# Half-size products of Strassen's scheme in the out-projection and the MLP of a decode-step kernel

## What is computed

```
x = x + gate1 * (concat(pool_out, attn_out) @ w_out)          # w_out 1024 x 1024
h2 = rmsnorm(x, g_mlp) * (1 + scale2) + shift2
x = x + gate2 * (square(relu(h2 @ w_up)) @ w_down)            # 1024 x 4096, 4096 x 1024
y = rmsnorm(x, g_final)
```

## Time and profile before

| | us |
|---|---|
| median of 3 runs (1449.72 to 1454.08) | 1452.13 |
| span of the profiled execution | 1451.2 |
| TensorE (PE) busy | 1406.3 |
| VectorE (DVE) busy | 692.3 |
| ScalarE (ACT) busy | 397.4 |
| GpSimd (POOL) busy | 373.8 |

### The profile page before, as it was taken

One profiled execution on the slowest core, in us unless ns is written; L12 is line 12 of the kernel. 1 busy time (PEld: TensorE's weight loads), 2 busy tenths in 40 slices (PEclk: granted clock), 3 DMA queues, 4 the chain that ended last, 5 costly groups with the idle time before them and its releaser, 6 DMA issues.

```text
span 1451.2 us, 25502 instructions
## 1 busy us (share of the span) xinstructions
PE 1406.3 (97%) x10814; PEld 1283.6 (88%) x10814; DVE 692.3 (48%) x1358; ACT 397.4 (27%) x875; POOL 373.8 (26%) x278
## 2 busy tenths in 40 slices
PE   6999999999989998999999999999999999999998
PEld 4899876667667766999999999999999999999997
DVE  4846655655657776476532332322323323223245
ACT  5521655555413333323301102011021020110244
POOL 0032042222312217110614306025051060330400
PEclk9999989999979999999999999999999999999999
DMA  9612234234657755400211203003021030120102
GB/s 350 258 51 61 93 103 139 96 112 144 191 210 255 248 205 150 159 16 15 75 43 51 66 1 102 15 16 101 1 73 44 1 103 15 44 73 1 44 15 110
DMA packets 93920, 139.65 MB, mean 96 GB/s; under 512 B 14027, under 2 KB 65175, under 8 KB 89575
## 3 DMA queue, kind: packets, MB, share of 16 engines
q1 hardware_dynamic: 83701, 95.74, 20.6%
q0 software_dynamic: 5760, 37.75, 7.3%
q10 hardware_dynamic: 4346, 4.54, 1.0%
HBM read 121.98 MB, written 13.79 MB: 94 GB/s over the span
## 4 chain that ended last, share of the span: by engine, by line
PE 89%; DVE 4%; DMA 3%; issue 2%; ACT 1%; POOL 0%; SPq 0%; DVEq 0%; ACTq 0%
PE psa L1263 26%; PE psa L1277 26%; PE psa L1241 6%; PE psa L795 4%; PE psa L1135 4%; PE psa L979 3%; PE psa L861 3%; PE psa L1185 3%; PE psa L1017 2%; PE psa L1000 2%; DMA wm<-in_w_mod 2%; PE psa L400 1%; PE psa L876 1%; PE psa L1167 1%; PE psa L918 1%
## 5 line engine op out<-in xcount | busy, mean ns | idle before, releaser
L1263 PE MATMUL psa<-hhi,wr 128*128 128x384 f32 (+1 forms) x1536 | 374.5, 326 | 0.0
L1263 PEld LDWEIGHTS psa<-hhi,wr 128*128 128x128 f32 x1536 | 270.8, 188 | 0.1
L1277 PE MATMUL psa<-g_hi,wd_hi 128*128 128x384 f32 (+1 forms) x768 | 251.3, 327 | 0.0
L1263 PE MATMUL psa<-hlo,wr 128*128 128x384 f32 (+1 forms) x768 | 250.3, 326 | 0.0
L1277 PE MATMUL psa<-g_hi,wd_lo 128*128 128x384 f32 (+1 forms) x768 | 250.3, 326 | 0.0
L1277 PE MATMUL psa<-g_lo,wd_hi 128*128 128x384 f32 (+1 forms) x768 | 250.2, 326 | 0.0
L2184 DVE SCALAR_TENSOR_TENSOR xT<-psa,modT,xT 128x384 f32<-128x384 f32 (+1 forms) x216 | 123.1, 571 | 191.8 <-PE psa L1277 160.6
L1703 ACT ACTIVATE g_relu<-psa 128x384 f32<-128x384 f32 (+1 forms) x96 | 45.4, 473 | 600.9 <-PE psa L1263 600.9
L590 POOL TENSOR_SCALAR wr<-wraw 128x1024 fp32r<-128x1024 f32 x33 | 34.8, 1054 | 558.1 <-PE psa L1263 487.9
L2248 DVE TENSOR_TENSOR psa<-psa,g_relu 128x384 f32<-128x384 f32 (+1 forms) x96 | 52.2, 543 | 261.7 <-ACT g_relu L1703 261.7
L1263 PEld LDWEIGHTS psa<-hlo,wr 128*128 128x128 f32 x768 | 144.1, 188 | 0.1
(11 more groups left out here) (305 smaller groups left out, 2225.1 us busy)
## 6 DMA issues: line engine op xcount, KB each, us to landing
wmod<-in_w_mod SPq DMA_DIRECT2D x8, 2048.0 KB, 8.5
wraw<-in_w_up SPq DMA_DIRECT2D x32, 512.0 KB, 4.1
wraw<-in_w_down SPq DMA_DIRECT2D x32, 512.0 KB, 3.5
wm<-in_w_mod SPq DMA_DIRECT2D x4, 2048.0 KB, 19.5
x_scr<-xT SPq DMA_DIRECT2D x1, 4352.0 KB, 19.6
wraw<-in_w_out SPq DMA_DIRECT2D x8, 512.0 KB, 4.2
out_y_p<-yst SPq DMA_DIRECT2D x8, 512.0 KB, 2.6
xstage<-in_x_prompt SPq DMA_DIRECT2D x3, 1024.0 KB, 10.5
```

Of the source, the lines that this page charges most:

```text
L1263: mm = pe.matmul(out[:, :N], w[:, c * P:c * P + P], x[:, c, c0:c0 + N], start=(c == 0 and q == 0), stop=(c == KD - 1 and q == 2))
L1277: mm = pe.matmul(out[:, :N], w[:, c, n * P:n * P + P], x[:, c, c0:c0 + N], start=(c == 0 and q == 0), stop=(c == FG - 1 and q == 2))
```

## The change

The out-projection and the MLP become nine stages of the same size: stage 0 is the out-projection, and then four times an up stage (1024 of the 4096 columns) and a down stage. Each stage is a product of a 1024 x 1024 weight block and a 1024 x 1088 activation block, done by one level of Strassen's scheme in Winograd's form: the weights in four quarters of 512 x 512, the activations in two halves of rows and two token halves of 544 (`HT`). Seven products M1 to M7 of quarters (some of them sums of quarters) take the place of eight. Each product is a phase of four steps, one for each 128 rows of the half-size contraction; a step is 24 matmuls with 272 columns (`HB`): two token quarters, four output tiles, three products of high and low parts. The eight output tiles of a phase fill all eight PSUM banks. M2, M1 and M5 open new sums; M6, M7 and M4 go on from M1, and M3 from M5, in the same banks, after the sum so far was read.

For every step, a piece of weights (128 x 512) and a piece of activations (128 x 544) are made anew: `w_sum` on POOL forms the sum of weight quarters where the product wants one, `w_high` on ACT the high part, `w_low` on POOL the low part; `x_sum` on DVE, `x_high` on ACT and `x_low` on DVE do the same for the activations. All of `w_sum`, `w_low`, `x_sum` and `x_low` read two SBUF operands. There are four slots for the high and low parts: the high part of step j waits until step j - 4 is done. The sums run one step ahead of the low parts in POOL's and DVE's lists.

After each phase its eight tiles are read (`kept`): in the even stages (out, down) by `residual` on DVE; in the odd ones (up) by ACT (`first_kept`, after M2, M6, M7 and M4) or by `added` on DVE (after M1, M5 and M3), into `g_all`, which `activated` on DVE then turns into relu squared in place. In DVE's list the reading of a phase stands behind the low parts of the first three steps of the next phase. Each unit of the next phase's first step waits for the reading of its bank. The old functions `split_wo`, `split_up`, `split_down`, `wo_unit`, `up_unit`, `down_unit`, `cat_high`, `cat_low`, `norm_high`, `norm_low`, `up_high` and `relu_low` go. The norm between stage 0 and stage 1 works by token halves instead of by three blocks, and the final norm, the last turns and the stores are arranged anew for tiles of 64 to 120 tokens. Weights are loaded as whole quarters of 1 MB. The core of the diff, with the new functions:

```
+HT, HB = T // 2, T // 4
+STAGES = 9
+STEPS = 28
+EARLY = ('M2', 'M1', 'M6', 'M7', 'M4', 'M5', 'M3')
+LATE = ('M5', 'M3', 'M1', 'M6', 'M7', 'M4', 'M2')
+ORDERS = (LATE,) + (EARLY,) * (STAGES - 2) + (LATE,)
+OPENS = ('M2', 'M1', 'M5')
+TARGET = {'M2': (0, 0), 'M1': (0, 0), 'M6': (0, 1), 'M7': (1, 1), 'M4': (1, 0), 'M5': (1, 1), 'M3': (0, 1)}
+W_SUMMED = [('M5', 'M3', 'M7') if o is LATE else ('M6', 'M7', 'M5', 'M3') for o in ORDERS]
...
+X_SUMMED = ('M5', 'M6', 'M7', 'M4')
...
+    def tail_bank(p, i):
+        return bank(i if p else 4 + i)
...
+            before = w - 2 if name == 'A12' else w - 1
+            if before >= 0:
+                sp.wait_ge(sem("w_low"), STEPS * before + 4 * LAST_USE[name][before] + 4)
+            k = quarter_slot(w, name)
+            sp.dma_start(quarters[k][:, :, :], src).then_inc(sem(f"quarter_in{k}"), 16)
...
+        def w_sum(j):
+            w, pos, k, m = place(j)
+            if m not in W_SUMMED[w]:
+                return
+            a11, a12, a21, a22 = (w_quarter(w, name, k) for name in ('A11', 'A12', 'A21', 'A22'))
+            s2 = s2_sum[:, k, :]
+            if ORDERS[w] is LATE:
+                if m == 'M5':
+                    s = g.tensor_tensor(s2, a21, a22, ALU.add)
+                elif m == 'M3':
+                    chain(g.tensor_tensor(s2, s2, a11, ALU.subtract))
+                    s = g.tensor_tensor(s4_tmp[:, k % 2, :], a12, s2, ALU.subtract)
+                else:
+                    s = g.tensor_tensor(a11, a11, a21, ALU.subtract)
+            elif m == 'M6':
+                chain(g.tensor_tensor(s2, a11, a21, ALU.subtract))
+                s = g.tensor_tensor(s2, a22, s2, ALU.subtract)
+            elif m == 'M7':
+                s = g.tensor_tensor(a11, a11, a21, ALU.subtract)
+            elif m == 'M5':
+                s = g.tensor_tensor(a21, a21, a22, ALU.add)
             else:
+                s = g.tensor_tensor(s2, a12, s2, ALU.subtract)
+            s.then_inc(sem("w_sum"), 1)
+        def w_low(j):
+            if place(j)[3] in W_SUMMED[place(j)[0]]:
+                g.wait_ge(sem("w_sum"), BEFORE["w_sum"] + W_SUMS[j])
+            g.wait_ge(sem("w_high"), j + 1)
+            g.tensor_tensor(w_lo[j % 4][:, :], w_piece(j), w_hi[j % 4][:, :].bitcast(F32), ALU.subtract).then_inc(sem("w_low"), 1)
...
+            for q, (a, x) in enumerate(products(w_hi[s], w_lo[s], x_hi[s], x_lo[s])):
+                mm = pe.matmul(tail_bank(p, i)[:, 0:HB], a[:, i * P:i * P + P], x[:, HB * p:HB * p + HB],
+                               start=(m in OPENS and k == 0 and q == 0), stop=(k == 3 and q == 2),
+                               skip_group_check=True)
...
+        def step(j, p):
+            phase, k = j // 4, j % 4
+            pe.wait_ge(sem("w_low"), j + 1)
+            pe.wait_ge(sem("x_low"), j + 1)
+            for i in range(4):
+                if k == 0 and phase:
+                    pe.wait_ge(sem("unit_kept"), 8 * (phase - 1) + unit_rank(phase - 1, p, i) + 1)
+                if k == 0 and p == 0 and i >= 2 and phase in (6, 8):
+                    pe.wait_ge(sem("n_root"), phase // 2 - 2)
+                mm = unit_part(j, p, i)
+                if k == 3:
+                    mm.then_inc(sem("unit_mm"), 1)
...
+        def total(n):
+            pe.wait_ge(sem("n_sum"), n + 1)
+            pe.wait_ge(sem("unit_kept"), 8 * (6 + 2 * n))
+            for e in range(2):
+                c0 = HT * n + HB * e
+                mm = pe.matmul(bank(6 + e)[:, 0:HB], ones[:, :], h_all[:, 0, c0:c0 + HB], start=True, stop=True)
...
+        for j in range(4, 4 * (7 * STAGES - 1)):
+            if j == 24:
+                total(0)
+            if j == 32:
+                total(1)
+            step(j, 1)
+            mm = step(j, 0)
+            if j % 4 < 3:
+                mm.then_inc(sem("step_mm"), 1)
...
+        def w_high(j):
+            w, pos, k, m = place(j)
+            if j >= 4:
+                wait_step(act, j - 4)
...
+            act.activation(w_hi[j % 4][:, :], w_piece(j), ACT.Copy).then_inc(sem("w_high"), 1)
...
+            act.activation(x_hi[j % 4][:, :], x_piece(j), ACT.Copy).then_inc(sem("x_high"), 1)
...
+        def first_kept(phase):
+            for n in range(8):
+                out, c, c0, u = unit_tile(phase, n)
+                act.wait_ge(sem("unit_mm"), u + 1)
+                act.activation(g_all[:, c, c0:c0 + HB], out[:, 0:HB], ACT.Copy).then_inc(sem("unit_kept"), 1)
...
+            if j % 4 == 3 and w % 2 and m in ('M2', 'M6', 'M7', 'M4'):
+                first_kept(phase)
...
+        def x_sum(j):
...
+            if m == 'M5':
+                s = tt(x_piece(j), b12, b11, ALU.subtract)
+            elif m == 'M6':
+                chain(tt(t2, b22, b12, ALU.subtract))
+                s = tt(t2, t2, b11, ALU.add)
+            elif m == 'M7':
+                s = tt(x_piece(j), b22, b12, ALU.subtract)
+            else:
+                s = tt(t2, b21, t2, ALU.subtract)
+            s.then_inc(sem("x_sum"), 1)
...
+        def x_low(j):
+            if place(j)[3] in X_SUMMED:
+                v.wait_ge(sem("x_sum"), X_SUMS[j])
+            v.wait_ge(sem("x_high"), j + 1)
+            tt(x_lo[j % 4][:, :], x_piece(j), x_hi[j % 4][:, :].bitcast(F32), ALU.subtract).then_inc(sem("x_low"), 1)
...
+        def residual(phase, n):
+            w = phase // 7
+            out, c, c0, u = unit_tile(phase, n)
+            N, gate = HB, (M_G2 if w else M_G1) + c
+            if phase:
+                v.wait_ge(sem("unit_kept"), u - 7)
+            if c0 == TP + TS - HB:
+                N = HB - TS
+                if u:
+                    v.wait_ge(sem("unit_kept"), u)
+                new = xT[:, c, TP:T].rearrange("p (b s) -> p b s", b=NB)
+                gates = modT[:, gate, 1:9].unsqueeze(2).to_broadcast([P, NB, NS])
+                chain(tt(tmp_s[:, :, :], out[:, N:HB].rearrange("p (b s) -> p b s", b=NB), gates, ALU.mult))
                 tt(new, new, tmp_s[:, :, :], ALU.add)
+            v.scalar_tensor_tensor(out=xT[:, c, c0:c0 + N], in0=out[:, 0:N], scalar=modT[:, gate, 0:1], in1=xT[:, c, c0:c0 + N],
+                                   op0=ALU.mult, op1=ALU.add).then_inc(sem("unit_kept"), 1)
...
+        def added(phase, n):
...
+            tt(g_all[:, c, c0:c0 + HB], out[:, 0:HB], g_all[:, c, c0:c0 + HB], ALU.add).then_inc(sem("unit_kept"), 1)
...
+        def activated(phase, i):
...
+            v.scalar_tensor_tensor(out=cols, in0=cols, scalar=0.0, in1=cols, op0=ALU.max, op1=ALU.mult).then_inc(sem("g_done"), 1)
...
+        def kept(phase):
...
+            for n in range(8):
+                if w % 2 == 0:
+                    residual(phase, n)
+                elif m in ('M1', 'M5', 'M3'):
+                    added(phase, n)
...
+        for j in range(4, STAGES * STEPS):
+            phase = (j - 7) // 4
+            w, m = phase // 7, ORDERS[phase // 7][phase % 7]
+            if j % 4 == 3:
+                kept(phase)
+                if phase in (7 * STAGES - 9, 7 * STAGES - 8):
+                    for i in range(4):
+                        activated(phase, i)
+            if j % 4 < 2 and j >= 8:
+                phase = (j - 8) // 4
+                w, m = phase // 7, ORDERS[phase // 7][phase % 7]
+                if phase not in (7 * STAGES - 9, 7 * STAGES - 8) and w % 2 and m in ('M1', 'M4', 'M5', 'M3'):
+                    activated(phase, 2 * (j % 4))
+                    activated(phase, 2 * (j % 4) + 1)
+            if j in (25, 33, 249):
+                add_squares({25: 0, 33: 1, 249: 2}[j])
+            if j == 35:
+                x_low(35)
+                inverse(1)
+                sample_scale(v, chain, h_all[:, :, TP:T], xT[:, :, TP:T], rr[:, TP - HT:HT], A2, M_SH2).then_inc(sem("h_samples"), 1)
+                for c in (4, 0, 5, 1):
+                    scale_h(1, c)
+                x_sum(36)
+                continue
+            if j in (36, 37):
+                scale_h(1, j - 30)
+                scale_h(1, j - 34)
+            if j + 1 < STAGES * STEPS:
+                x_sum(j + 1)
+            x_low(j)
+            if j == 27:
+                inverse(0)
+                scale_h(0, 4)
+                scale_h(0, 5)
+            if 28 <= j < 34:
+                scale_h(0, (6, 7, 0, 1, 2, 3)[j - 28])
```

## The result

The changed kernel takes 1595.89 us (median of four runs, 1590.94 to 1599.36) against 1453.11 before (four runs): ratio 1.0988, interval 1.0959 to 1.1017, slower. The profiled execution has a span of 1596.4 us, 145.2 above the 1451.2 of before. The forecast was 62 more.

A forecast was written before the change was run, and what follows sets the result against it. PE's own rate was taken to bound the kernel before. 756 + 57.6 + 34.4 + 18.4 + 32 + 18 + 8 + 5 = 929.4 us in place of 867.6: 62 more, 1513; range 1383 to 1555.

The forecast's parts named there:

- Products: All nine stages: 6048 matmuls of 272 columns at 125 ns, 63 phases of 12.0 us, 756 us against 853.
- Turns: DVE and POOL operations on two SBUF operands alternate: round 1.72 us; up stage 92 us, down stage 83, PE needs 84.
- M1 to M6: PE's wait for DVE's bank reading while M6 is prepared: 10.8 us in down stages, 7.6 in up stages.
- Down stages: PE waits 19.2 us in each: 10.8 after M1, 3.5 M6, 1.4 M7, 1.7 M4, 1.8 M5 and M3; 57.6 for three.
- Tiles with sample tokens need 0.39 for the small operations: DVE's reading of banks with sample tokens: 0.39 us plus 0.43 for the main operation; with four such, eight take 5.0.
- Up stages: PE waits 8.6 us in each of four, 34.4 together: 7.6 around M6's preparation and about 1 for the relu squares.
- The relu squares add about 1: In up stages, DVE's squared ReLU operations add about 1 us of waiting to the 7.6, making 8.6 each.
- Stages 0 and 1: Waits with the norm and the start, 54 us; includes 8.7 for stage 0, 32 for the second norm, 5 for the start.
- Stage 8 and the end: Last down stage's waits of 9.7 us and the end's 8, taken as before: 17.7 us.
- Clock: About nine PE waits of 7 us or more each bring some 5 us at half clock, costing 2 each: 18 us.
- turns hardly bite: Rival: DVE and POOL fall into each other's gaps, 1385 us, faster; chance 0.23 for 1370 to 1415.
- The weight load binds: Rival: weight loads bind matmuls at 272 columns, since PEld is busy for 88%; no chance of its own.

The follow-up runs named there:

- the kernel with both edits: Changed kernel with the sample part's temporary in PSUM and DVE's reading of a phase's banks one step earlier in its list: 1507.67 us, ratio 1.0395 to before.
- the sample part's edit: Changed kernel with the gated sample part in spare PSUM columns instead of an SBUF buffer, and the wait on the residual before dropped: 1541.85 us, ratio 1.0609.
- the filler run: Changed kernel with 100 small 128x128 matmuls on TensorE ahead of the third product M6 in stages 1 to 7: 1586.46 us; output not the same.
- run 22: No run has this label; the words come from "In the filler run 22 us of clock went", where 22 us is a time and the run is the filler run.
- four tries: M6's sums moved earlier on the shared-difference kernel (1467.62 us), then three re-placements, each with left halves, the last with ACT's reading earlier: 1464.51, 1458.26, 1453.22, 1453.20 us.
- the version level with before: Second re-placement of M6's sums on DVE, on top of squared ReLU on ACT, shared difference and left halves in the last phase: 1453.22 us, ratio 1.0001.

## Why the prediction was wrong

The direction, the mechanism and the place were right. The time came out 83 us above the forecast and 41 above the range. Term by term, forecast against measured:

- **Products**, 756 us: right (126 ns apart for 125).
- **Turns**: round 1.72 us, measured 1.74. The Trainium skill's page "SBUF — State Buffer" (section "SBUF: two separate sides") has the shared port pair held for the whole instruction; that an operation waits out the other's whole one agrees with the 32-column sum of 1273 ns. The round by that rule, the two full durations (1.29 and 0.73, together 2.02), does not come out: five rounds took 8.72 us.
- **M1 to M6**: forecast 10.8 in down stages and 7.6 in up stages; PE's gaps there are 10.5 and 7.9. Right.
- **Down stages**, 57.6 for three: measured waits 65.1. The step that failed is "Tiles with sample tokens need 0.39 for the small operations". It was read from a row of a stretch in which POOL had no work. The add has two SBUF operands, so the prediction's own rule applies to it: 635 ns in the mean, not 225; 31 of the 76 took 224 or 225 ns, the others 0.49 to 1.31 us. It shows where such tiles are read: PE waits 3.5 us at M4 (forecast 1.4) and 6.4 at M3 and the next stage's M2 together (forecast 1.8). With the temporary in PSUM these are 0.8 and 1.9. The 3.5 at M7 came out (3.7), and the 1.7 at M5 erred to the other side (0.3). The runs with it put 40 us of time on the add, with the clock behind it and stages 0 and 8 among them, and 14 on the wait between tiles.
- **Up stages**, 8.6 each: 15.4, 15.5 and 18.6 in stages 3, 5 and 7. Ahead of M6 it is 7.9 (forecast 7.6). "The relu squares add about 1" failed: 1.6 us stand ahead of M7 and 2.9 ahead of M3. On DVE the squares average 1373 ns, and taking them off, from the kernel with both edits, gave 4 to 7.5 us a stage. Another 2.8 stand at the stage's start and belong to the sample tiles of the down stage before (0.7 with the temporary in PSUM); stage 7 has 3.2 more at the change to stage 8.
- **Stages 0 and 1** with the norm and the start, 54: measured 53. Right in sum, which may be luck: 18.2 of them stand in one wait, ahead of M6 in stage 1, and the parts were not tested one by one.
- **Stage 8 and the end**, 17.7: 32.3. I left out that the final norm's sums of squares (`add_squares(2)`) stand in DVE's list in this stage, and that the last phase waits for all banks of the one before. Of the 32.3, 17 stand in the first six phases (forecast 9.7) and 15.3 in the last (forecast 8). With DVE's work short this stage fell from 127.8 to 112.1, in the first six phases; the last kept 15.2 us of waits, and what sets them was not tested.
- **Clock**, 18 with bounds 0 and 25: 56. Eight waits of 7 us or more came and lost some 16 us in all, the 2 each that were forecast. What failed is that "about nine waits of 7 us or more" were taken for all of it: there are 33 stretches at 0.50, since pauses of 1.4 to 3 us at the head of a phase have one behind them as well, though not always, and the other 40 us stand there. 18 of the stretches went with the sample part's edit. In the filler run 22 us of clock went with 9 to 16 us of time, with a filler that itself held PE up.

The terms that failed add up: 7.5 + 24 (6.8, 6.9 and 10.0 in the three up stages) + 14.6 + 38, less 1 for stages 0 and 1, make 83.

The rival "turns hardly bite" fell: 1385 asked for two-operand operations near 0.73 us, and that took POOL's work away. "The weight load binds" fell with the starts 126 ns apart. The range was too narrow at the upper end: the norm, the clock, the start and the end had bounds, but the waits of the down stages, of the up stages and of stage 8 had none. The small terms (sample part, relu, clock, end) all erred to one side, and they hang together: more waits at the heads of phases mean more time at half clock (the sample part's edit gave 27 us of waits and 30 of clock).

Open: what the single waits in stages 0, 1 and 8 are worth. Moving PE's column sums gained 3 us in stage 8 and lost as much in stages 0 and 1, and no other edit of the norm's chain was tried.

## What to carry to other kernels

A scheme that saves matmuls and pays with elementwise sums has to be costed on the engines that do the sums, and together: where DVE and POOL both work on SBUF operands, add up the turns of both over a stage and hold that against TensorE's time. A small operation with two SBUF operands is to be counted too, with a wait of up to the other engine's whole operation (45 of the 76 adds had one here); one operand in PSUM takes it out. When the sum of turns is near TensorE's time, taking operations away pays (squared ReLU on ACT, a shared difference, a temporary in PSUM), while moving the sums about mostly moves the wait (four tries gave 3, 6, 5 and 0 us, the second with another edit in it). In an engine's list, the reading that frees a buffer should not stand behind preparation that is needed later (one step earlier gave 44 us).

## What the runs showed of the hardware

- A DVE operation of 32 columns on two SBUF operands took 1273 ns beside POOL's 512-column operations and 182 ns without them. A 64-column add took 635 ns in the mean, 227 with POOL's operations cut to 32 columns, and 224 with one operand in PSUM beside whole POOL operations.
- With POOL's operations cut to 32 columns DVE's 544-column low parts, whole, took 729 ns in place of 1301, and stages 4 and 5 ran at a clock of 1.00.
- Pauses of PE of 1.4 to 3 us were often followed by a stretch of 3.4 or 6.8 us at 0.50; three of 1.6 to 1.7 us ahead of M7 and one of 2.89 us were not. Between the first product and the last the changed kernel spent 195 us of 1012 at that level, the version level with before 51 us of 866.
